# Another order of ScalarE's copies in the attention part of a hybrid decoder layer

## The reference

```
h = rmsnorm(x);  xa, ga, q, k, v, gate_a, gate_b = split(h @ w_in)
branch_a = (rg_lru(causal_conv(xa)) * gelu(ga)) @ w_br_a
q, k = rmsnorm per head;  3 groups x 4 heads x 128, windows/dilations (128,1) (512,4) (2048,16)
for g in 3 groups: o_g, lse_g = dilated_attention(q_g, k_ext_g, v_ext_g)     # k_ext: cached keys, then new ones
att = sum_g softmax(lse)_g * o_g;  branch_b = att @ w_br_b
x = x + (sigmoid(gate_a) * branch_a + sigmoid(gate_b) * branch_b) @ w_out
x = x + (gelu(conv(up_g)) * conv(up_v)) @ w_down       # up = rmsnorm(x) @ w_up, 1024 -> 6144 -> 1024
outputs: both x, the recurrent and convolution states, and the keys and values
```

## Time and profile before

| | |
|---|---|
| Median of 3 runs | 1207.9 us (1207.88 to 1209.78) |
| Profiled execution, device time | 1207.88 us |
| Its span in the profile | 1206.1 us |
| PE busy | 1190.7 us (99%) |
| PE weight loads busy | 1159.3 us (96%) |
| DVE busy | 659.5 us (55%) |
| ACT busy | 457.8 us (38%) |
| POOL busy | 160.3 us (13%) |
| Passes over the heads | about 20 to 353 us |
| Gate units | about 353 to 412 us |

### The profile page before, as it was taken

One profiled execution on the slowest core, in us unless ns is written; L12 is line 12 of the kernel. 1 busy time (PEld: TensorE's weight loads), 2 busy tenths in 40 slices (PEclk: granted clock), 3 DMA queues, 4 the chain that ended last, 5 costly groups with the idle time before them and its releaser, 6 DMA issues.

```text
span 1206.1 us, 21188 instructions
## 1 busy us (share of the span) xinstructions
PE 1190.7 (99%) x8793; PEld 1159.3 (96%) x8793; DVE 659.5 (55%) x1330; ACT 457.8 (38%) x709; POOL 160.3 (13%) x250
## 2 busy tenths in 40 slices
PE   9999999999999999999999999999999999999998
PEld 7989999999999999999999999999999999999998
DVE  6554443543532346575645457888428884378831
ACT  6434444434433356757533344222212222122221
POOL 2265134143131000000010020000100001000010
PEclk9999999999999999999999999999999999999999
DMA  8565245245232222222162222333232222222231
GB/s 242 139 183 161 78 121 163 76 121 148 76 94 71 59 82 70 72 87 62 46 198 76 75 82 71 88 86 87 75 87 84 74 86 83 79 87 83 74 102 52
DMA packets 182948, 117.14 MB, mean 97 GB/s; under 512 B 6932, under 2 KB 175528, under 8 KB 182856
## 3 DMA queue, kind: packets, MB, share of 16 engines
q1 hardware_dynamic: 172320, 89.70, 26.5%
q0 software_dynamic: 10544, 26.43, 7.9%
q10 hardware_dynamic: 10, 0.01, 0.0%
HBM read 107.66 MB, written 8.45 MB: 96 GB/s over the span
## 4 chain that ended last, share of the span: by engine, by line
PE 94%; DMA 2%; DVE 2%; POOL 1%; ACT 1%; issue 0%; ACTq 0%; DVEq 0%
PE ps L628 64%; PE ps L607 18%; PE ps L760 2%; PE ps L837 1%; DMA kc<-in_cache_k_g 1%; PE ps L724 1%; PE ps L698 1%; PE ps L738 1%; PE ps L685 1%; DMA w_raw<-in_w_br_a 1%; PE ps L765 1%; PE ps L899 0%; PE ps L710 0%; PE ps L650 0%; POOL kc L476 0%
## 5 line engine op out<-in xcount | busy, mean ns | idle before, releaser
L628 PE MATMUL ps<-h,w_s 128*128 128x288 f32 x3840 | 518.6, 297 | 0.0
L628 PEld LDWEIGHTS ps<-h,w_s 128*128 128x128 f32 x3840 | 513.3, 189 | 1.2 <-issue 0.2
L1324 DVE TENSOR_TENSOR w_s<-w_raw,w_s 128x1024 fp32r<-128x1024 f32 (+1 forms) x161 | 195.7, 1216 | 198.8 <-ACT w_s L955 198.0
L955 ACT ACTIVATE w_s<-w_raw 128x1024 fp32r<-128x1024 f32 (+1 forms) x161 | 167.4, 1040 | 351.0 <-PE ps L628 347.4
L607 PE MATMUL ps<-w_s,h 128*128 128x384 f32 x1152 | 217.5, 341 | 1.3 <-DVE h L1354 0.8
L607 PEld LDWEIGHTS ps<-w_s,h 128*128 128x128 f32 x1152 | 198.8, 188 | 3.4 <-issue 1.7
L628 PE MATMUL ps<-g_hi,w_s 128*128 128x288 f32 x768 | 136.3, 297 | 1.6 <-DVE g_lo L1758 1.6
L628 PEld LDWEIGHTS ps<-g_hi,w_s 128*128 128x128 f32 x768 | 113.5, 189 | 1.9 <-ACT g_hi L1288 1.8
L628 PE MATMUL ps<-g_lo,w_s 128*128 128x288 f32 x384 | 82.2, 296 | 0.0
L628 PEld LDWEIGHTS ps<-g_lo,w_s 128*128 128x128 f32 x384 | 61.9, 189 | 0.0
L569 POOL DMA_DIRECT2D out<-f_row x12 | 6.2, 518 | 414.4 <-ACT f_row L1295 414.4
(11 more groups left out here) (285 smaller groups left out, 1413.4 us busy)
## 6 DMA issues: line engine op xcount, KB each, us to landing
w_raw<-in_w_in SPq DMA_DIRECT2D x65, 512.0 KB, 4.0
w_raw<-in_w_up SPq DMA_DIRECT2D x48, 512.0 KB, 3.9
w_raw<-in_w_down SPq DMA_DIRECT2D x24, 512.0 KB, 3.8
kc<-in_cache_k_g POOLq DMA_DIRECT2D x48, 128.0 KB, 3.0
vc<-in_cache_v_g POOLq DMA_DIRECT2D x12, 512.0 KB, 6.1
w_raw<-in_w_br_a SPq DMA_DIRECT2D x8, 512.0 KB, 4.0
w_raw<-in_w_out SPq DMA_DIRECT2D x8, 512.0 KB, 3.9
x_tok<-in_x_prompt SPq DMA_DIRECT2D x4, 512.0 KB, 7.4
```

Source lines behind the costliest of these rows:

```text
L628: last = mm(pu[u % 2][:, 512 * a:512 * a + HALF], w[:, part, k, :], x[:, k, HALF * a:HALF * (a + 1)], start=(k == 0 and i == 0), stop=(k = ...
L955: A(w_s[:, ring(u), 0, 0:nkt[u], :], w_raw[:, u % NRAW, 0:nkt[u], :], ACT.Copy).then_inc(hi_ready, 1)
L1324: TT(w_s[:, ring(u), 1, 0:nkt[u], :], w_raw[:, u % NRAW, 0:nkt[u], :], w_s[:, ring(u), 0, 0:nkt[u], :], ALU.subtract).then_inc(lo_ready, 1)
```

## The change

Only ScalarE's queue is written in another order; the programs of the other engines stay the same, and so do all buffers and semaphores. Three things move.

```
                     if hp and s == 6:
                         take_out(hp - 1, 4)
-                    if prev and s == 5:
-                        take_out(hp - 1, 3)
                     if s in (5, 10):
                         sample_stat(hp, s // 10)
                         root_of(hp, s // 10)
@@
-                    if prev and 2 <= s < 5:
+                    if prev and s >= 2:
                         take_out(hp - 1, s - 2)
                     split_ahead(hp, s)
-                    if s == 13:
-                        take_cached_T(hp, 3)
                     if hp == 0 and s == 11:
                         softplus()
                     if s == 14:
-                        for b in (5, 7):
+                        for b in (3, 5, 7):
                             take_cached_T(hp, b)
@@
             for m in range(KT):
                 if m == 0:
                     take_rows(NSLOT * NH - 1)
-
+                else:
+                    hi_split(U_GA + m + 1)
+                    gate_raw(U_GA + m - 1, sg_a[:, m - 1, :])
                 if 1 <= m <= 5:
                     take_probs_T(NH - 1, m - 1)
-                if m:
-                    hi_split(U_GA + m + 1)
                 if 2 <= m <= 6:
                     take_out(NH - 1, m - 2)
                 if m < 5:
                     exps(NH - 1, m)
-                if m:
-                    gate_raw(U_GA + m - 1, sg_a[:, m - 1, :])
```

## The result

| | before | changed |
|---|---|---|
| Median of 5 runs | 1207.88 us | 1215.72 us (1212.98 to 1219.02) |
| Median of all 17 executions on record | | 1214.99 us |
| Ratio to before, from the 17 | | 1.0059, 95% interval 1.0043 to 1.0076 |
| Profiled execution / its span | 1207.88 / 1206.1 us | 1215.19 / 1213.4 us |
| PE, ACT busy | 1190.7, 457.8 us | 1191.9, 457.6 us |

The account below looks back on a forecast made before the run. The prediction took the kernel to be bound by a queue of TensorE instructions with hardly a gap. New waits of 2.7, 1.9 and 1.5 us sum to 6.1 us on 1207.88, giving 1214.0 us, range 1212.2 to 1217.2.

Parts of the forecast that it names:

- Gate units: Units 2 to 5: O waits for the later probT copy, three times 0.75 and once 0.46 us; 2.7 us taken.
- Tile 5: Passes 1 to 3: V4 waits for O3's output copy behind the statistics, 0.63 us each; 1.9 us.
- A0: Tile 14, four passes: starts 1.24 us later behind T3's copy, partly replacing transfer waits; sum 1.5 us.
- the shorter of the two cases: Tile 5: copy to att starts 0.11 us before L1029's end, V4 at 220.43, 0.57 us later.
- Rival (a): Tile 14: cached-key transfers move along with A0 through shared DMA engines, no wait is replaced; 1217.5 us, chance 0.07.
- (b): Later stages: PE's waits of 1.6 and 1.0 us and 1.0 us idle shrink; 1210.4 us, chance 0.05.
- (c): Gate units: splits up to 1.3 us earlier carry a lead to later weight waits; 1205.3 us at best, chance 0.02.
- (d): Gate units: pauses lower TensorE's clock to 1.2 GHz, 13.7 us more; 1227.7 us, chance 0.02.
- the forecast of the wait list: PE's waits: L777 0.75 three times and 0.46, L760 0.63, L710 1.24 us; L698 falls from 4.9 to 1.5.
- The range: Whole kernel: 1212.2 to 1217.2 us, from the sum's low ends to high ends without transfers moving, plus 1.9 scatter.

Follow-up runs that it names:

- e3: The kernel before with only the gate-unit part: weight split and gate copy ahead of the copy to probT; 1210.68 us, ratio 1.0016.
- e4: The kernel before with only the gate units' weight split moved ahead of the probT copy, gate copy left last; 1209.38 us, ratio 0.9998.
- e7: The kernel before with only the gate units' gate copy moved ahead of the probT copy, split left behind it; one execution, 1206.09 us.
- e1: The kernel before with only the copy of O3's output moved behind the key statistics, tile 5 of passes 1 to 3; 1209.68 us, ratio 1.0008.
- e2: The kernel before with only the copy of T3 moved behind the copy of tile 13's rows; 1209.26 us, ratio 1.0011.
- e9: The kernel before, ScalarE's old order, with TensorE's O, V4, A0 and T4 to T7 in later blocks; 1206.44 us, ratio 0.9979.
- e5: The whole changed kernel with TensorE's O, O3, V4, A0, T4 to T7 and B0 in later blocks; 1206.04 us, ratio 0.9982.
- e8: The kernel before with T0 to T3 transposed earlier and VectorE's copy of T0 ahead of its weight split; 1206.95 us, ratio 0.9988.
- e10: The kernel before, old ScalarE order, with TensorE's later steps, early transposes of T0 to T3 and early T0 copy; 1205.84 us, ratio 0.9976.

## Why the prediction was right

The forecast was 1214.0 us, 6.1 above before. The ratios are 1.0059 and 1.0051, 7.1 and 6.2 us, and the first profile has 6.13 us at the end of the gate units. The mechanism is the forecast one. How closely the total fits is partly luck, since transfers and start-up move by as much as the terms in question.

- **Gate units, 2.7 forecast.** 2.77 us to O3 in the first profile (0.75, 0.77, 0.76, 0.49), 2.79 in e3. The mechanism is shown by e4 and e7: each of the two moved instructions had the price that start-to-start distances and the slack gave.
- **Tile 5, 1.9 forecast.** 1.94 in e1, 0.63 to 0.67 a pass in the changed kernel. The statistics start 0.71 behind the probT copy (0.70 forecast), and the copy to `att` starts 0.10 before the recorded end of L1029, as in the shorter of the two cases; the rest is that V4's matmuls start slower after a wait. VectorE's o_sb is 0.73 later, of which O3 already had 0.65.
- **A0, 1.24 each forecast.** 1.28 to 1.39: A0 starts 0.21 us behind the end of T3's copy (0.30 in pass 2), where I had put 0.15, the distance seen at O3. In passes 0 to 2 it took the place of waits for the transfer, with nothing left in passes 0 and 1 and 0.11 in pass 2 (0, 0.07 and 0.21 forecast), and 1.28 in pass 3: 1.4 us where 1.5 was forecast. My transfer waits were taken from the bracket of the rows, which is too short: T6 follows T4 by 1.92 us in pass 3, and by 3.25 in pass 1, so the wait was 1.33, not 1.17. By the same spacing pass 2's was 1.20 and the two of pass 0 were 1.2 and 1.9. The size of this term rests on one execution, though. In e1, e3, e4 and e7, which leave tiles 12 to 14 alone, T6 of pass 2 waited only 0.17, 0.01, 0.00 and 0.07 us, while pass 1 kept 1.4 to 1.9. In such an execution nothing takes up A0's 1.3 us of pass 2, and the term is about 2.6 us (an estimate: passes 2 and 3 in full). That it came out at 1.4 goes with the profile of before that I subtracted.
- **Rival (a)**, transfers move along: refuted by e2 and by the 0.2 us left in the changed kernel. **(b)**, later waits take it up: no later wait shrank. Its price was also wrong: the idle 1.0 us between 617 and 622 is the wait at sg_b, which it had counted already, so it could have saved 2.6 us and not 3.6. **(c)**, earlier splits give a lead: e9 against e5 shows no such gain. **(d)**, the clock: windows of the changed kernel over the first stretch of the earlier trace rows, and over the gate units, still have 1.00 as the granted clock:

```profile
84.00:97.00 13.00, 11.53 (x109) 9.95 (x108) 3.07 (x8) 2.96 (x6) 9.50 (x17) 1.00 0.71 189
360.00:412.00 52.00, 49.98 (x419) 47.05 (x418) 13.26 (x39) 17.86 (x33) 7.17 (x10) 1.00 0.25 65
```

  The mean granted clock of its 23 executions was 0.9991, that of 81 executions of the kernel before 0.9986, so the added waits, 1.3 us at most, did not lower it. But I had taken (d) too lightly as a mechanism: in e3 and e4 the clock did fall, at waits of 2.3 to 3.3 us, while in the changed kernel it stayed at 1.00 through waits of 2.27 and 2.22 us.

- **What the forecast of the wait list had wrong.** It expected 0.75 and 0.63 as waits; the list has 0.5 to 0.6 and 0.4. The displacement was right, and the list counts less, because a row's time on PE runs past the start of the next matmul (345.17 + 2.89 = 348.06 against A0's 347.98 in the earlier trace rows). It also left 1.5 us of transfer waits in pass 0, and 0.2 were found: most of it had been taken up by the start-up, 1.4 us late in this execution. That is not the whole account, as e2 also had none left with a start-up only 0.4 us late.
- **The range.** Its ends are off by 0.2 and 0.1 us against its own terms: 1207.9 + 4.5 is 1212.4, not 1212.2, and 1215.4 + 1.9 is 1217.3.
- **The scatter.** 1.22 us of the profiled 7.3 are the wait at sg_b, which no term held. It varies between executions.

  Much of the scatter of totals goes with the clock. Of the kernel before, executions with a mean granted clock of 1.000, 0.999 and 0.997 have medians of 1207.2, 1208.6 and 1211.7 us (18, 34 and 10 of them). Compared at the same clock the changed kernel is 7.0 us slower at 1.000 and 6.4 at 0.999 (10 and 7 executions, 1214.2 and 1215.0 us).

  The three parts alone sum to 1.0035, the whole is 1.0051 and 1.0059; with intervals of 0.0013 to 0.0019 on each, the gap doesn't show that the parts cost more together, and doesn't exclude it. A straight line in the clock, fitted to all these executions (1.2 us for 0.001), gives e1 1.2, e2 1.4 and e3 2.4 us, each within 0.8, and the whole 6.7 within 0.6. This estimate leaves a gap of 1.7, within 1.6: a hint that the whole costs a little more than its parts (the executions came from more than one chip, which the line leaves out of account). The traces show no wait for it apart from the one at sg_b, and it stays open.

## What to carry to other kernels

On an in-order helper engine, price a reordering by one subtraction for each consumer: when the result is there now (the gate, plus start-to-start distances, plus the hand-over), less when the bound engine arrives. Work that fits ahead of the result's own input is free, and what sticks out is paid in full. If the bound engine can be given other work first, as in e5, the order of the helper stops mattering; and where it already waits for a transfer a little later, a new wait only takes that wait's place. Look at more than one profile before you count on such a wait: the one of pass 2 was there in one execution and missing in four others.

## What the runs showed of the hardware

A single execution of this kernel moves by several us where nothing was changed. T0 of pass 0 started between 0.1 us earlier and 4.1 us later than before (without e8 and e10, where T0 itself is moved). About 1.6 of the 4.1 us, in e3, came with a stretch of granted clock 0.50. The landing of the transfers of cached keys and of branch a's weights (the sg_b wait, 1.0 to 2.8 us) moved too. In pass 0 a late start-up is partly taken up by the transfer waits, so two profiles can agree at 110 us and have been 1.4 us apart at 76.

The granted clock of this single-core kernel is not always 1.00. It fell to 0.50 in e3 and e4, at waits of 2.27, 2.8 and 3.30 us. It did not fall at waits of 2.27 us (changed) and 2.2 us (changed, e10). The same wait for VectorE's `h`, 2.27 us long, had a fall behind it in e3 and none in the changed kernel, so its length alone does not decide it here. Over the executions of the kernel before, 0.003 of mean clock go with 4.4 us.

In the rows shown ScalarE starts its next instruction 0.09 to 0.11 us before the recorded end of the one before. TensorE's O and V4 start 0.14 or 0.15 us behind the end of the copy that they wait for, and A0 0.21 us (once 0.30), in all profiles that have these waits.
